# GpSimd adds four chunks of squares, and TensorE sums what is left behind the first early panel

## What is computed

```python
def rmsnorm(x, w):
    xf = x.astype(jnp.float32)
    y = xf * lax.rsqrt(jnp.mean(xf * xf, axis=-1, keepdims=True) + EPS)
    return (y * w.astype(jnp.float32)).astype(x.dtype)
...
for layer in range(DEPTH):                       # DEPTH = 2
    x = x + 0.5 * swiglu(rmsnorm(x, norm_ffn1[layer]), ...)      # D_FF = 2816
    x = x + hybrid_mixer(rmsnorm(x, norm_mix[layer]), ...)
    x = x + 0.5 * swiglu(rmsnorm(x, norm_ffn2[layer]), ...)
x = rmsnorm(x, norm_final)
...
u = rmsnorm_2(h, g_pre_mix[i])                   # second block, one layer
...
h = h + rmsnorm_2(mixed @ w_o[i], g_post_mix[i])
v2 = rmsnorm_2(h, g_pre_mlp[i])
h = h + rmsnorm_2(f, g_post_mlp[i])
gate = jax.nn.sigmoid(rmsnorm_2(h, g_pre_ple[i]) @ w_ple_gate[i] + b_ple_gate[i])
h = h + rmsnorm_2(gate * e, g_post_ple[i])
```

## Time and profile before

| | |
|---|---|
| median of three runs | 2089.42 us (2088.04 to 2096.73) |
| profiled execution | span 2084.0 us from the first to the last instruction; its own time is not listed apart, and the median of the runs is 5.4 us above the span |
| PE busy | 1912.0 us (92%) |
| DVE busy | 1144.4 us (55%) |
| ACT busy | 948.9 us (46%) |
| POOL busy | 158.0 us (8%) |
| mean granted TensorE clock | 0.951 |

### The profile page before, as it was taken

How to read it: one execution, slowest core, us unless ns; L and a number is a source line. 1 busy time by engine, 2 the same in 40 slices (tenths; PEclk the granted TensorE clock), 3 DMA queues, 4 the chain that set the end, 5 groups by cost and what they waited for, 6 DMA issues and landing times.

```text
span 2084.0 us, 33803 instructions
## 1 busy us (share of the span) xinstructions
PE 1912.0 (92%) x14848; PEld 1861.5 (89%) x14848; DVE 1144.4 (55%) x1352; ACT 948.9 (46%) x945; POOL 158.0 (8%) x120
## 2 busy tenths in 40 slices
PE   7999878889999999968989999999899999889987
PEld 7999877789999999867879998999799889789986
DVE  5544859555446444767746445543356435555555
ACT  6333654354335333646255334544544333444445
POOL 0000221000000000051000000690000000000000
PEclk9999988989999999988989999999999869999998
DMA  7555431025554555442024554555244404435541
GB/s 238 169 184 184 142 101 61 21 82 182 182 182 162 183 183 183 151 120 83 1 82 162 182 183 162 160 182 173 78 145 163 142 0 142 142 127 182 183 162 41
DMA packets 219842, 291.01 MB, mean 140 GB/s; under 512 B 4560, under 2 KB 197200, under 8 KB 219440
## 3 DMA queue, kind: packets, MB, share of 16 engines
q1 hardware_dynamic: 219248, 287.08, 42.4%
q0 software_dynamic: 448, 1.77, 0.3%
HBM read 287.78 MB, written 1.05 MB: 139 GB/s over the span
## 4 chain that ended last, share of the span: by engine, by line
PE 76%; DVE 11%; ACT 7%; issue 3%; POOL 3%; DMA 0%; SPq 0%; ACTq 0%; DVEq 0%
PE colb L754 46%; PE acc L754 26%; DVE w_lo L1362 3%; PE aux L754 3%; ACT w_hi L1084 3%; POOL arena L623 1%; DVE u L1422 1%; PE colb L1030 1%; DVE x L1465 1%; POOL arena L624 1%; POOL arena L620 0%; DMA raw<-ffn_gate 0%; DVE op_lo L1428 0%; ACT L1141 0%; DVE op_lo L1417 0%
## 5 line engine op out<-in xcount | busy, mean ns | idle before, releaser
L1362 DVE TENSOR_TENSOR w_lo<-raw,w_hi 128x2048 fp32r<-128x2048 f32 x271 | 625.4, 2308 | 600.5 <-ACT w_hi L1084 600.0
L1084 ACT ACTIVATE w_hi<-raw 128x2048 fp32r<-128x2048 f32 x271 | 515.5, 1902 | 373.1 <-PE acc L754 234.5
L754 PE MATMUL colb<-u_hi,w_hi 128*128 128x256 f32 x2256 | 647.2, 287 | 39.9 <-DVE w_lo L1362 34.6
L754 PE MATMUL colb<-u_lo,w_hi 128*128 128x256 f32 x2256 | 643.7, 285 | 0.0
L754 PE MATMUL colb<-u_hi,w_lo 128*128 128x256 f32 x2256 | 643.5, 285 | 0.0
L754 PEld LDWEIGHTS colb<-u_hi,w_hi 128*128 128x128 f32 x2256 | 438.8, 194 | 43.8 <-issue 38.0
L754 PEld LDWEIGHTS colb<-u_lo,w_hi 128*128 128x128 f32 x2256 | 438.7, 194 | 0.1
L754 PEld LDWEIGHTS colb<-u_hi,w_lo 128*128 128x128 f32 x2256 | 438.5, 194 | 0.0
L754 PE MATMUL acc<-op_hi,w_hi 128*128 128x256 f32 x1328 | 384.1, 289 | 37.0 <-DVE op_lo L1417 27.6
L754 PE MATMUL acc<-op_lo,w_hi 128*128 128x256 f32 x1328 | 381.5, 287 | 0.0
L754 PE MATMUL acc<-op_hi,w_lo 128*128 128x256 f32 x1328 | 381.2, 287 | 0.0
(11 more groups left out here) (289 smaller groups left out, 2045.9 us busy)
## 6 DMA issues: line engine op xcount, KB each, us to landing
raw<-w_in SPq DMA_DIRECT2D x78, 1024.0 KB, 5.1
raw<-ffn_gate SPq DMA_DIRECT2D x44, 1024.0 KB, 5.3
raw<-ffn_up SPq DMA_DIRECT2D x44, 1024.0 KB, 5.4
raw<-ffn_down SPq DMA_DIRECT2D x44, 1024.0 KB, 4.9
raw<-w_up SPq DMA_DIRECT2D x16, 1024.0 KB, 5.4
raw<-w_down SPq DMA_DIRECT2D x16, 1024.0 KB, 5.0
raw<-w_out SPq DMA_DIRECT2D x8, 1024.0 KB, 4.9
raw<-w_ret_out SPq DMA_DIRECT2D x8, 1024.0 KB, 4.9
```

The lines of the kernel that those rows point to most:

```text
L754: return pe.matmul(o, a, b, start=start, stop=stop, skip_group_check=True)
L1084: act.activation(split_view(w_hi, r), raw[:, p % RAW_SLOTS, 0:r["kt"] * r["nc"]], ACT.Copy)\
L1362: tt(split_view(w_lo, r), raw[:, p % RAW_SLOTS, 0:r["kt"] * r["nc"]], split_view(w_hi, r).bitcast(F32), ALU.subtract).then_inc(sem("w_lo_r ...
```

## The change

In the nine norms that feed a product, POOL adds chunks 1, 2 and 3 of the squares onto chunk 0 as they come, three additions of 128 x 512. PE then has two slices of `sq` left to sum in place of eight, and it does so in a new step, `norm_total`, that stands behind the first early panel in the list. The four other norms stay as they are.

```diff
@@ -278,6 +278,8 @@
             panels.append(r)
             schedule.append(("panel", r))
+            if r.get("half") == 0:
+                step("norm_total", n=r["norm"], k=r["fill"]["n"])
             return r
@@ -677,6 +679,18 @@
+            added = [0]
+
+            def norm_sum(r):
+                if r["next"] != "fill":
+                    return
+                for b in range(1, 4):
+                    pool.wait_ge(sem("sq_ready"), 4 * (r["n"] - 1) + b + 1)
+                    tt(sq[:, 0:2, :], sq[:, 0:2, :], sq[:, 2 * b:2 * b + 2, :], ALU.add).then_inc(sem("sq_added"), 1)
+                    added[0] += 1
+                    if b < 3:
+                        pool.wait_ge(sem("sq_added"), added[0])
+
@@ -798,9 +812,17 @@
-            def norm_sum(r):
+            def norm_total(r):
                 if r["n"] == 1:
                     pe.wait_ge(sem("ones_set"), 1)
+                pe.wait_ge(sem("sq_added"), 3 * r["k"])
+                for i in range(2):
+                    last = mm(aux[:, 0:T], ones, sq[:, i, :], i == 0, i == 1)
+                last.then_inc(sem("norm_summed"), 1)
+
+            def norm_sum(r):
+                if r["next"] == "fill":
+                    return
                 for kk in range(KD):
```

More of the change, by code:

```diff
@@ L742, in load_p @@
                 pool.dma_start(p32, ap["p_t"]).then_inc(sem("p_loaded"), 16)
-            run = {"gate_rows": gate_rows, "rg_scan": rg_scan, "ret_tables": ret_tables, "rope": rope, "dil_tables": dil_tables,
+            run = {"norm_sum": norm_sum, "gate_rows": gate_rows, "rg_scan": rg_scan, "ret_tables": ret_tables, "rope": rope, "dil_tables": dil_tables,
                    "load_p": load_p}
@@ L1057, in dil_end @@
                 last.then_inc(sem("dil_o_turned"), 1)
-            run = {"panel": gemm, "norm_sum": norm_sum, "gd_ss": gd_ss, "rg_gates": rg_gates,
+            run = {"panel": gemm, "norm_sum": norm_sum, "norm_total": norm_total, "gd_ss": gd_ss, "rg_gates": rg_gates,
                    "spread": spread, "gd_scores": gd_scores, "gd_x0": gd_x0, "gd_y": gd_y, "gd_z": gd_z,
```

## The result

The changed kernel takes 2150.34 us, median of 4 runs (2144.84 to 2153.96), beside 2088.73 us (2083.92 to 2096.73) for the kernel before on the same chip: a ratio of 1.031, 95% interval 1.029 to 1.033, or 61.6 us slower. Its profiled execution took 2149.67 us, with a span of 2147.9 beside 2084.0, 63.9 us more. (Every run on record takes 1.8 us more than its own span. The 5.4 us that the prediction added came from setting the median of the runs beside the span of another execution.) Lines have moved: what was L1362 is L1384, L1428 is L1450, L1422 is L1444, L1465 is L1487, L1451 is L1473, L1084 is L1106, L1140 and L1141 are L1162 and L1163, L754 is L768; the additions are L689.

What follows compares the result with a forecast made beforehand. PE was taken to bound the kernel, with 76% of the chain, and the `rstd` chain to have zero slack. Norm costs of 4.3, 26.0, 9.6 and 2.5 summed to 42.4 us on 2089.4, giving 2132 us, range 2110 to 2150.

Steps and rivals of the forecast that it cites:

- The nine norms: Step adding the costs of the nine norms that feed a product: 42.4 us in all.
- second rival: POOL delays DVE at each addition and the clock falls at each norm: 61 us; more than 52 us had chance 0.08.
- The chain without slack, and rstd 2.4 us later: DVE and ACT's chain from `rstd` to the third panel has zero slack, so PE loses 2.4 us per norm.
- third rival: Unseen slack at the third panel lets PE keep its earlier start: some 7 us faster, 2082 us; chance 0.06.
- the first, late `rstd` alone: POOL yields to DVE and the clock stays up, leaving only the later `rstd`: 21.6 us, 2111 us; chance 0.2.
- The additions, d = 1.8: POOL's additions hold up DVE between first update and last gained chunk: 1.8 us per norm, bounds 0 and 3.2.
- The clock, c = 1.0: PE's clock may fall in the first early panel while waiting for chunks: 1.0 us per norm, bounds 0 and 2.0.
- Norms 2 to 6: Five norms, each paying 2.4 for late `rstd`, 1.8 for additions and 1.0 for the clock: 26.0 us.
- Norm 1: First early panel waits for weights; the sum behind it delays `rstd` and the third panel's split and end: 4.3 us.
- Norm 7: Same chain as at norms 2 to 6, PE arriving after a long idle time: 4.8 us.
- Both terms at their bounds: Additions at 3.2 and clock at 2.0 us per norm: 61 us, 2151 us; more than 52 us had chance 0.08.
- My +0.5 without additions: At norm 9 the third panel's split comes 1.5 us later and PE has 1 us to spare: 0.5 us lost.

Runs made afterwards that it cites:

- late_two_warm: Changed kernel without POOL's additions, only two of eight slices summed behind the first early panel, plus dummy matmuls in PE's waits at norms 2 to 9: 2113.08 us, ratio 1.010.
- after: The changed kernel itself, set against the kernel before: 2150.34 us, ratio 1.031.
- warm: The changed kernel plus dummy matmuls that nothing reads, in PE's waits at norms 2 to 9, to keep the clock up: 2130.42 us, ratio 1.022.
- split_first: The changed kernel with ACT's split of the second early panel ahead of Ln at norm 1 too: 2138.59 us, ratio 1.025.
- adds_only: The kernel before plus POOL's additions, written to a scratch tile that nothing reads, PE's order unmoved: 2101.72 us, ratio 1.009.
- front_two: The changed kernel with its additions, but the two sum matmuls ahead of the first early panel again: 2131.98 us, ratio 1.024.
- late_two: The changed kernel without POOL's additions; PE sums only two of eight slices behind the first early panel: 2104.51 us, ratio 1.012.
- again: The kernel before run once more, unchanged, for its profile: one time of 2080.48 us.

## Why the prediction was wrong in its size

The direction, the two main mechanisms and the missing slack were right. The time, 2150.3 us, lies just beyond the range (2150); two of its four runs lie inside. The predicted sum was 42.4 us, the measured one 61.6 (63.7 in the cells of the profiled execution). What failed is the step "The nine norms", which priced norms 1, 7 and 9 with too little of their own: they cost 8.3, 10.0 and 6.3 us for 4.3, 4.8 and 2.5, which is 13.0 of the 21.3 us that the cells have more than the sum. The clock's term was too small as well. That the measured 61.6 is the 61 of the second rival is luck: that rival needs 7.6 us at every norm from 2 to 8, and norms 2 to 6 cost 5.8. The terms stand so:

- **The chain without slack, and rstd 2.4 us later: right.** late_two_warm has the late sum with the clock up and no additions, and norms 2 to 6 cost 2.27 us each (from 2.00 to 2.42). The third rival, slack in the chain, is refuted by it, and the first, late `rstd` alone, was the right size for what it held (late_two_warm's cells outside the attention sum to 9.7 + 11.3 + 1.0 + 3.0 + 3.1 = 28, of which norm 1 is 9.7, beside the 21.6 predicted with 4.3 at norm 1).
- **The additions, d = 1.8: low.** DVE's stretch grew by 2.28 at norm 3, and by the difference of two kernels they cost 2.5 in the mean and 2.3 at norms 4 and 6. In the rows above the single `op_lo` product loses 1.06 us, the pair 0.91 and the scaling pair 0.30. The Trainium skill (SBUF — State Buffer, "Who interferes with whom") says that a DVE instruction with two SBUF inputs and a GpSimd one that reads SBUF exclude each other. By that rule the updates that read PSUM are spared, and the trace agrees: L1487 keeps its 0.68 to 0.69.
- **The clock, c = 1.0: too small where it can be told apart.** It is 1.6 and 2.1 at norms 4 and 6, and 1.7 in the mean without additions; after less warm gives 1.1, with warm's own clock down at norms 2, 3 and 5. The prediction had one fall, and at norm 3 there are two. The second is at the third panel, behind a wait that the change itself makes.
- **Norms 2 to 6: 29.2 for 26.0.**
- **Norm 1: 8.3 for 4.3.** This step failed. I took the third panel's chain from `rstd`, as at the other norms, but overlooked that at norm 1 alone the split of the *second* early panel stands behind Ln and Exp in ACT's list (the `+ (r["n"] > 1)` in `norm_sum`). ACT and DVE of the changed kernel at norm 1:

```profile
25.42 0.47 ACT L1162 ACTIVATE rstd<-aux,bias 128x256 f32<-128x256 f32 x1 [10.15 <-PE aux L768]
...
27.52 1.89 ACT L1106 ACTIVATE w_hi<-raw 128x2048 fp32r<-128x2048 f32 x1
```

```profile
29.45 2.29 DVE L1384 TENSOR_TENSOR w_lo<-raw,w_hi 128x2048 fp32r<-128x2048 f32 x1 [13.16 <-ACT w_hi L1106]
```

```profile
31.89 0.55 PE L768 MATMUL colb<-op_hi,w_hi 128*128 128x256 f32 x1 [6.51 <-DVE w_lo L1384]
```

  PE stands 6.51 us at the second early panel, one panel ahead of where I looked. The row at 25.06 in the earlier trace rows is the third panel's split, as I took it; the second's stands ahead of it, behind Exp, and I had shown no row of it. In the kernel before it cost nothing, since it began at 18.12 and the first early panel ended at 25.0:

```profile
17.79 0.42 ACT L1141 ACTIVATE rstd<-rstd 128x256 f32<-128x256 f32 x1
18.12 1.89 ACT L1084 ACTIVATE w_hi<-raw 128x2048 fp32r<-128x2048 f32 x1
```

  With the order mended (split_first) the loss is 4.9 to 5.9, near the 4.3 worked out.
- **Norm 7: 10.0 for 4.8.** This is the largest miss. There the update has two SBUF inputs, not one in PSUM, so all of DVE's instructions can be held, the update most:

```profile
1339.18 1.64 POOL L689 TENSOR_TENSOR sq<-sq 128x512 f32<-128x512 f32 x1 [204.23 <-ACT sq L1180]
```

```profile
1337.56 0.88 DVE L1491 SCALAR_TENSOR_TENSOR x<-x,cols,rstd 128x256 f32<-128x256 f32 x2
...
1339.61 1.89 DVE L1491 SCALAR_TENSOR_TENSOR x<-x,cols,rstd 128x256 f32<-128x256 f32 x2
```

  The pair takes 1.89 us beside the addition, 0.88 alone, and DVE's stretch is 2.95 us longer (11.40 for 8.45). The other part is the clock. In both kernels it falls about 2 us behind the norm's first square: before, behind a wait of PE of 3.95 us; after, within a wait of 6.07 us. Before, it is up again after 3.4 us. Here it stays down for 13.7 us, through the first early panel, and is down for 6.9 us more at the third panel:

```profile
1340.00:1352.00 12.00, 9.19 (x39) 8.31 (x40) 9.63 (x12) 5.61 (x6) 7.12 (x9) 0.50 0.26 70
```

  The late sum alone costs +0.8 to +1.0 there, adds_only +5.3, with 17.6 us more at the lower level, and warm gives back 5.2. front_two has the same additions and costs +3.5, with 6.9 us more at the lower level. So the differences between the kernels at this norm go in good part with the clock; how the 10.0 divides was not run.
- **Norm 8: 6.3 for 4.8; norm 9: 6.3 for 2.5.** At norm 8 all three additions run as one block of 4.66 us beside DVE's last pair. At norm 9 the update is again one with two SBUF inputs (1.78 for 0.69), and DVE's stretch grows from 7.68 to 10.80, almost the bound of 3.2 that I had taken as rare. My +0.5 without additions was too small too: late_two has +0.9 up to the last norm and 1.7 more behind it, late_two_warm has +3.1.
- **The attention: +4.8 and -1.2 for 0.** Not in the sum, and by "again" within what one execution differs from another.

The step that failed for the range was "Both terms at their bounds", 0.08 for more than 52 us: it let d reach 3.2 and c reach 2.0 at the norms, yet had nothing for norm 1's list, for two falls of the clock, or for updates without PSUM at norms 7 and 9. Against the sum, norm 1 has 4.0 us more, norms 2 to 6 have 3.2, norm 7 has 5.2, norms 8 and 9 have 5.3, and the attention's two cells the remaining 3.6.

## What to carry to other kernels

Work that is moved from a matmul engine to an idle GpSimd isn't free where DVE works without a gap on two-SBUF-input instructions: price it as DVE time on the path, and look at each place for which operands lie in PSUM. Before moving a sum later, read every engine's own list at each place where the pattern repeats; the one norm with another order cost 8.3 us, and 3.5 of them went when the order was mended. And a new wait of PE can be paid twice: once by its length, once by the matmuls behind it at the lower clock (late_two at norms 3, 5 and 6, but not at norm 4, where the clock stayed up). Last, look in the trace for the price of an operation before building on it: the reciprocal's was there.

## What the runs showed of the hardware

- A reciprocal on DVE of 128x256 f32 took 1.75 us (8x256: 1.74), where a product of 128x512 takes 0.69.
- The dilated attention, the same code in all kernels, took 38.1, 51.6, 52.8, 56.3 or 61.2 us, with 4.6, 33.8, 35.6, 43.8 and 54.0 us of it at the lower granted clock, while PE is shown as busy for all of the ten microseconds of the row at 0.50 above. That is up to 23 us in the total.
- ACT's load of the table for Ln went ahead of the wait for the sum at each of the nine norms of the changed kernel (480.26 at norm 3, with Ln at 485.71), so a late sum doesn't add its 1.28 us.
